# A hybrid decoder layer on one core: expert passes of 96 and 32 rows on four column tiles, two banks for head pairs, moved convolution taps, squares added ahead, and x transposed unscaled

## What is computed

```
h = rms_norm(x); proj = h @ w_in                     # conv value, conv gate, q, k, v
conv = silu(layer_norm(causal_conv31(value * sigmoid(gate))))    # 512 channels
attn = attention(rope(q), rope(k), v)                # 8 heads of 64, causal
x += concat(rms_norm(conv), rms_norm(attn)) @ w_out
h2 = rms_norm(x, g_ffn)
group = argmax(h2 @ w_group + b_group)               # 1 of 4
e1, e2 = top2(h2 @ w_erouter[group] + b)             # 2 of its 8 experts
x += sum of gate * (silu(h2 @ w_gate[e]) * (h2 @ w_up[e])) @ w_down[e]   # 32 experts, 1024 -> 256 -> 1024
x += (p @ w_ple) * sigmoid(rms_norm(x) @ w_ple_gate + b)
out = rms_norm(x, g_final)
```

## Time and profile before

| | us |
|---|---|
| median of 3 runs | 652.24 (651.92 to 652.33) |
| the profiled execution | 651.7 |
| its span, first to last instruction | 649.8 |
| PE busy in the span | 551.8 (85%) |
| DVE, ACT, POOL busy | 297.3, 185.7, 82.2 |
| mean granted PE clock | 0.945 of full speed |
| chain that ended last | PE 55%, DVE 19%, DMA 15%, ACT 7% |

### The profile page before, as it was taken

One profiled execution on the slowest core, in us unless ns is written; L12 is line 12 of the kernel. 1 busy time (PEld: TensorE's weight loads), 2 busy tenths in 40 slices (PEclk: granted clock), 3 DMA queues, 4 the chain that ended last, 5 costly groups with the idle time before them and its releaser, 6 DMA issues.

```text
span 649.8 us, 7753 instructions
## 1 busy us (share of the span) xinstructions
PE 551.8 (85%) x2628; PEld 322.9 (50%) x2629; DVE 297.3 (46%) x551; ACT 185.7 (29%) x348; POOL 82.2 (13%) x106
## 2 busy tenths in 40 slices
PE   1999999985779898897997889999999998729980
PEld 1788887753456687543332233333333332228870
DVE  3339868998872924474211111211121121175754
ACT  4831411346742432121101010110111010154554
POOL 0650000000000030002112012112211211000000
PEclk9999999996779989989999899999999999958995
DMA  8902102545004001664899998699899999265012
GB/s 342 384 3 72 67 9 58 219 144 211 1 0 195 1 1 66 266 283 168 323 418 419 421 421 348 235 419 385 335 417 422 368 421 419 119 259 210 2 43 86
DMA packets 34248, 145.86 MB, mean 224 GB/s; under 512 B 6576, under 2 KB 6832, under 8 KB 21808
## 3 DMA queue, kind: packets, MB, share of 16 engines
q1 hardware_dynamic: 27168, 133.70, 51.6%
q0 software_dynamic: 6480, 10.50, 4.4%
q10 hardware_dynamic: 576, 1.34, 0.5%
HBM read 142.90 MB, written 14.68 MB: 242 GB/s over the span
## 4 chain that ended last, share of the span: by engine, by line
PE 55%; DVE 19%; DMA 15%; ACT 7%; issue 2%; SPq 1%; POOL 0%; DVEq 0%; ACTq 0%; POOLq 0%
PE bank L1518 17%; DMA wring<-w_up_in 12%; PE bank L1266 10%; PE bank L1534 7%; DVE mix L888 6%; PE bank L1379 6%; PE bank L1563 2%; PE bank L1290 2%; DVE wring L946 2%; PE bank L1360 1%; PE bank L1497 1%; DMA c<-cst_in 1%; PE bank L1347 1%; PE bank L1444 1%; PE bank L1314 1%
## 5 line engine op out<-in xcount | busy, mean ns | idle before, releaser
L1518 PE MATMUL bank<-wring,arena 128*64 128x512 f32 x640 | 142.8, 599 | 13.7 <-SPq L506 12.0
L1518 PEld LDWEIGHTS bank<-wring,arena 128*64 128x64 f32 x640 | 46.2, 138 | 107.4 <-issue 90.1
L888 DVE SCALAR_TENSOR_TENSOR mix<-arena,pr,mix 128x512 f32<-128x512 f32 x120 | 81.5, 751 | 0.0
L1534 PE MATMUL bank<-wring,arena 128*64 128x512 f32 x320 | 73.1, 599 | 9.5 <-ACT arena L800 9.5
L1176 DVE TENSOR_TENSOR arena<-arena,bank 128x256 f32<-128x256 f32 x20 | 8.4, 422 | 148.7 <-ACT arena L797 148.7
L797 ACT ACTIVATE arena<-bank 128x256 f32<-128x256 f32 x20 | 7.7, 384 | 143.9 <-PE bank L1518 143.9
L1534 PEld LDWEIGHTS bank<-wring,arena 128*64 128x64 f32 x320 | 21.2, 136 | 48.5 <-issue 34.3
L1181 DVE COPY arena<-bank 128x512 f32<-128x512 f32 x20 | 13.8, 692 | 66.4 <-PE bank L1534 66.4
L1266 PE MATMUL bank<-hT_hi,win_hi 128*128 128x512 f32 x128 | 33.5, 398 | 1.5 <-DVE hT_lo L866 0.9
L803 ACT ACTIVATE arena<-bank 128x512 f32<-128x512 f32 x20 | 11.9, 597 | 75.8 <-PE bank L1534 75.8
L1266 PE MATMUL bank<-hT_lo,win_hi 128*128 128x512 f32 x128 | 31.6, 389 | 0.0
(11 more groups left out here) (203 smaller groups left out, 812.0 us busy)
## 6 DMA issues: line engine op xcount, KB each, us to landing
wring<-w_gate_in SPq DMA_DIRECT2D x32, 1024.0 KB, 10.4
wring<-w_up_in SPq DMA_DIRECT2D x32, 1024.0 KB, 12.7
wring<-w_down_in SPq DMA_DIRECT2D x32, 1024.0 KB, 15.6
wring<-w_in_in SPq DMA_DIRECT2D x5, 2048.0 KB, 19.1
wring<-w_out_in SPq DMA_DIRECT2D x2, 2048.0 KB, 8.0
wring<-y_d SPq DMA_DIRECT2D x8, 512.0 KB, 6.8
xs<-x_in SPq DMA_DIRECT2D x4, 512.0 KB, 7.5
xs<-x_in SPq DMA_DIRECT2D x1, 2048.0 KB, 8.0
```

Source lines behind the costliest of these rows:

```text
L888: ins = dve.scalar_tensor_tensor(out=mixc[:, mm, :], in0=u[:, mm, j:j + S], scalar=w, in1=mixc[:, mm, :], op0=ALU.mult, op1=ALU.add)
L1518: ins = pe.matmul(pb[2 + s][a * CAP:(a + 1) * CAP, :], xgT[:, s, k, a * CAP:(a + 1) * CAP], up_w(w, a)[:, :, k, :], start=(k == 0), stop=( ...
L1534: ins = pe.matmul(pb[6 + half][a * CAP:(a + 1) * CAP, :], hidT[:, s, k, a * CAP:(a + 1) * CAP], dn_w(w, a)[:, k, half * 512:(half + 1) * 5 ...
```

## The change

What it does, part by part (`...` marks what is left out):

- Expert passes have room for 96 rows of one expert and 32 of the other, on four column tiles of 32. In pairs 0 and 1 the even expert is the one with room for 96; in pairs 2 to 15 it is the one with more rows, and SP reads from `order` which expert's weights go into which half of the slot. Each matmul of a pass becomes four.
- The head pairs' outputs lie in banks 6 and 7 in turn. ACT does `probs_out` before `attn_out`, and the split of the convolution half's output weights after the loop.
- Taps: 71 are done before the first scores (66), then 7 in each of the first four units (as before), one in each later one (two), and the last 13 after the loop (6). The first `turn` comes after 57 taps (44).
- POOL adds up the squares of the head pairs, DVE those of the convolution blocks, so that one product per token tile sums them; DVE no longer reduces 16 sums.
- PE turns x as it is, right after its additions; the router's weights are multiplied by the gains once (`wr_scaled`), logits come out with tokens on partitions, and DVE applies the row's scale and the bias (which goes over memory to be spread over partitions). The normalised rows are still stored for the gathers, off this path; the last tile's after the choice of experts.
- `outa` uses banks 0, 1, 2, 6, 7, 0, 1, 2, `outc` banks q % 3; the mean comes after q = 2; w_pp is loaded after the last `outa`.

```diff
-GLU2, GLU3, TURN, EARLY = 20, 34, 54, 66
-TAPS_BY = (73, 80, 87, 94) + tuple(range(96, 120, 2))
+GLU2, GLU3, TURN, EARLY = 20, 34, 57, 71
+TAPS_BY = (78, 85, 92, 99) + tuple(range(100, 112))
-CAP = 64
+BIG, SMALL = 96, 32
+PARTS = tuple((lo, lo + SMALL, lo // BIG) for lo in range(0, P, SMALL))
+FIXED = 2
+FAR_ON = 64
-MOST = PAIRS + 2 * S // CAP
+MOST = PAIRS + 2 * S // SMALL
-STEPS = S // CAP - 1
+STEPS = S // SMALL - 1
...
-            banks.use(("attn", u // TT), 6)
-    banks.use("attn_sq", 7)
+            banks.use(("attn", u // TT), 6 + u // TT % 2)
+    banks.use("attn_sq", 4)
...
+            def expert(g, a):
+                if isinstance(g, int) and g < FIXED:
+                    return 2 * g + a
+                return number(sp, order[0:1, bass.ds(g, 1), a], 0, NE - 1)
...
-                                 src[bass.ds(2 * g + a, 1)].rearrange("e (p k) n -> p (e k) n", k=DK)
+                                 src[bass.ds(expert(g, a), 1)].rearrange("e (p k) n -> p (e k) n", k=DK)
...
+                if m >= 1:
+                    pool.wait_ge(sqa_ready, m + 1)
+                    wait(pool, sq_added, m - 1)
+                    pool.tensor_tensor(sqa[:, 0, :], sqa[:, 0, :], sqa[:, m, :], ALU.add).then_inc(sq_added, 1)
...
-                if u_ == 9:
-                    act.wait_ge(woc_loaded, 16)
-                if 9 <= u_ < 9 + CM:
-                    split_out(0, u_ - 9)
+                if u_ >= 2:
+                    probs_out(u_ - 2)
                 if u_ % TT == 3 and u_ > TT:
                     attn_out(u_ // TT - 1)
-                if u_ >= 2:
-                    probs_out(u_ - 2)
             attn_out(CM - 1)
...
+                banks.wait_full(act, ("h2", t, 1))
+                emptied(act.activation(hT[:, 4:8, t * P:(t + 1) * P], ..., ACT.Copy), ("h2", t, 1))
...
-            taps(GLU3 - 6, TURN - 10)
+            taps(GLU3 - 6, TURN)
             turn(0)
-            taps(TURN - 10, TURN)
+            dve.tensor_tensor(wr[:], wr[:], ..., ALU.mult).then_inc(wr_scaled, 1)
             taps(TURN, EARLY)
...
-            for q in range(2):
+            for q in range(3):
                 add_scaled(("outa", q), 1, q)
...
+            for m in range(1, CM):
+                dve.wait_ge(osq_ready, m + 1)
+                wait(dve, csq_added, m - 1)
+                dve.tensor_tensor(sqc[:, 0, :], sqc[:, 0, :], sqc[:, m, :], ALU.add).then_inc(csq_added, 1)
...
+            def logits_out(t):
+                banks.wait_full(dve, "logit")
+                return dve.scalar_tensor_tensor(out=lg[:, t, :], in0=bk("logit")[:, t * NR:(t + 1) * NR], scalar=rs[:, 1, t:t + 1],
+                                                in1=bias_row, op0=ALU.mult, op1=ALU.add)
...
+            scaled_rows(1, TT - 1)
...
-            chosen_value(SIDE, table8(C_SIDE, NE))
...
+            step(dve.tensor_copy(beyond[:], bk("count")[:, 0:NE]))
+            step(dve.tensor_tensor(larger[:, FIXED:, 0], pairs[:, FIXED:, 0], pairs[:, FIXED:, 1], ALU.is_ge))
+            step(dve.tensor_scalar(larger[:, FIXED:, 1], larger[:, FIXED:, 0], -1.0, 1.0, ALU.mult, ALU.add))
+            step(dve.tensor_scalar(pairs, larger[:], float(1 - BIG // SMALL), float(BIG // SMALL), ALU.mult, ALU.add))
+            emptied(dve.tensor_tensor(pairs, pairs, tokens, ALU.mult), "count")
...
+            step(dve.tensor_scalar(LOW, T0, float(FAR_ON), None, ALU.is_lt))
+            dve.scalar_tensor_tensor(out=H, in0=LOW, scalar=float(FAR_ON), in1=T0, op0=ALU.mult, op1=ALU.add)
+            step(dve.tensor_scalar(T1, LOW, float(BIG // SMALL - 1), 1.0, ALU.mult, ALU.add))
+            step(dve.tensor_tensor(T1, T1, R, ALU.mult))
+            step(dve.tensor_tensor(cmp8, over8(T1, STEPS), table8(C_THR, STEPS), ALU.is_ge))
+            step(dve.tensor_reduce(X, cmp8, AX.X, ALU.add))
+            dve.tensor_tensor(H, H, X, ALU.add)
+            step(dve.tensor_scalar(T1, LOW, float(SMALL - BIG), float(BIG), ALU.mult, ALU.add))
+            step(dve.tensor_tensor(T1, T1, X, ALU.mult))
+            step(dve.tensor_tensor(T1, R, T1, ALU.subtract))
+            step(dve.scalar_tensor_tensor(out=KEY, in0=LOW, scalar=float(BIG), in1=T1, op0=ALU.mult, op1=ALU.add))
...
-                    for m in range(CM):
-                        ins = pe.matmul(bk(name)[:, t:t + 1], src[:, m, t * P:(t + 1) * P], ones[:, 0:1],
-                                        start=(m == 0), stop=(m == CM - 1))
+                    ins = pe.matmul(bk(name)[:, t:t + 1], src[:, t * P:(t + 1) * P], ones[:, 0:1], start=True, stop=True)
...
-                if u_ >= 2 * TT and u_ % TT == 0:
-                    attn_squares(u_ // TT - 2)
...
+            def turn_rows(t):
+                for half in range(2):
+                    banks.wait_emptied(pe, ("outc", 2 * t + half))
+                rows = xs[:, t, :].rearrange("p (n k) -> p k n", k=DK)
...
+            def logits(t):
+                for k in range(DK):
+                    if k % 4 == 0:
+                        banks.wait_emptied(pe, ("h2", t, k // 4))
+                    ins = pe.matmul(bk("logit")[:, t * NR:(t + 1) * NR], hT[:, k, t * P:(t + 1) * P], wr[:, k, :],
+                                    start=(k == 0), stop=(k == DK - 1))
...
-                if q == 1:
+                if q == 2:
                     pe.wait_ge(tap_done, CM * TAPS)
                     mean_of("mean", mixc)
...
+                if q == 1:
+                    pe.wait_ge(csq_added, CM - 1)
+                    channel_sum("conv_sq", sqc[:, 0, :])
+                if half == 0 and t >= 1:
+                    turn_rows(t - 1)
                 if half == 1 and t >= 1:
-                    turn_rows("h2", t - 1, TT)
+                    logits(t - 1)
+            turn_rows(TT - 1)
+            logits(TT - 1)
...
                 for k in range(DK):
-                    for a in range(2):
-                        ins = pe.matmul(pb[2 + s][a * CAP:(a + 1) * CAP, :], xgT[:, s, k, a * CAP:(a + 1) * CAP],
-                                        up_w(w, a)[:, :, k, :], start=(k == 0), stop=(k == DK - 1))
+                    for lo, hi, a in PARTS:
+                        ins = pe.matmul(pb[2 + s][lo:hi, :], xgT[:, s, k, lo:hi], up_w(w, a)[:, :, k, :],
+                                        start=(k == 0), stop=(k == DK - 1))
```

202 lines of the change are left out of this document (93 added, 109 removed).

## The result

The changed kernel takes 635.66 us (median of 4 runs, 633.76 to 638.25); the kernel before, run beside it, takes 652.08 (650.49 to 652.33). The ratio is 0.976, with a 95% interval of 0.971 to 0.980: 16.4 us faster, where 29 were forecast and the range allowed 613 to 641. The profiled execution took 638.25 us, the slowest of the four; its span is 636.1, its mean granted clock 0.933.

A forecast was written before the change was run, and what follows sets the result against it. Bounds by stage: waits and lowered clock in attention, VectorE then PE in output projection, VectorE in routing, PE or transfers in the expert loop. Gains 17.2 + 10.6 - 3.1 + 4.4 took 651.7 to 622.6 us; range 613 to 641.

The forecast's parts named there:

- the two rivals with 640 and 630: 640: four tiles overlap imperfectly, 0.13 us a group, chance 0.08; 630: clock stays low in attention, chance 0.15.
- the main case: Whole kernel: all terms as summed, 622.6 us, with bounds 616 to 629; chance 0.66.
- Attention: Attention loop: two banks, ScalarE's order and moved taps end the last `attend` at 179.8 instead of 199.7, gain 19.9 us.
- the walk through the units: Attention loop from unit 8 to the last `attend`: following each score through its steps gives 26.7 us, plus 2.5 for clock.
- Mean and first `outc`: Output projection: the mean after q = 2 costs 2.7 us, so the first `outc` ends 17.2 us earlier.
- The new bank order only lets PE run ahead of it: nothing: Output projection: changed banks let PE run ahead of VectorE's chain from mean to scaled convolution, for no gain.
- Squares and x unscaled: From `outc` to logits: net gain 1.4 us inside `outc`, 9.2 behind it, together 10.6, bounds 7 and 12.
- Routing: Choice of experts: added small operations 2.1 us, longer thresholds and lists 1.0, cost 3.1 on the path, bounds 2 and 5.
- Four tiles: Expert passes: a group of four column tiles takes what two take, price 0, upper ends 0.17 and 0.44 us a group.
- that rival: Expert passes: four tiles overlap imperfectly, 0.13 us a group, a pass of 15.5, total 640; chance 0.08.
- The expert loop: Passes: 18 run instead of 20, last down product ends at 563.5 instead of 567.9, gain 4.4 us.
- transfers bind from pair 5 on: 375.5 + 10 x 16.2: Expert loop: last weights come at 537.5 at 16.2 us a pair, plus 1 for the pause at pair 7.

The follow-up runs named there:

- E1: The changed kernel with all head pairs' outputs back in bank 6; 645.64 us, ratio 0.985 to the kernel before.
- the second profile: The changed kernel run again unaltered, on another chip; 635.92 us, ratio 0.975 to the kernel before.
- E4: The kernel before with each matmul of a pass cut to run on four column tiles of 32, same rows and passes; 655.27 us, ratio 1.002.
- E5: The changed kernel with SyncE reading a pair's two expert numbers once instead of before each of six transfers; 634.81 us, ratio 0.974.
- E2: The changed kernel with the old tap schedule (44 before the first rotation, 66 before the first scores, two per later unit); 646.03 us, ratio 0.986.
- E12: The changed kernel with expert numbers read once, low weight parts split before the mean, 17 passes and seven unread products on PE; 619.54 us, ratio 0.951.
- E3: The changed kernel with the passes of before: 64 rows of each expert, two column tiles, 20 passes, shorter routing; 628.2 us, ratio 0.960.
- E7: The changed kernel with 17 passes, fixed for these inputs, instead of 18 run two by two; 624.22 us, ratio 0.957.
- E10: The changed kernel with passes of 64 and 64 rows and VectorE's low output-weight parts split before the mean; 625.68 us, ratio 0.959.

## Why the prediction was right in its direction and too large

The forecast's number was 13 us too low, and its range held. Of the signs that it named, one went against it: it called itself wrong if the loop lasted longer than 264 us, and the loop lasted 270.7. The measured time lies nearer to the two rivals with 640 and 630 than to the main case, but for other reasons than theirs: no product on four tiles was slower, and the clock in the attention loop was 0.93, not under 0.8.

**Attention (19.9 forecast, 18.9 measured): right.** The wait for bank 6 was the cause named, E1 brings it back with its lowered clock, and what was late next was the rotated rows, as forecast. The shares were not what I thought: undone alone, the bank costs 7.8 us, the taps 9, ScalarE's order 4.5. They add up to 21.3, more than 18.9, so they overlap. I had costed the moved taps by the earlier start of the loop alone; but the walk through the units, 26.7 us, rested on the small number of taps in them, and that is where most of the taps' worth was.

**Mean and first `outc` (17.2 forecast, 14.7 measured).** The mean came 16.0 us earlier, as the one product more costs 2.9. The step that failed is "The new bank order only lets PE run ahead of it: nothing", and with it the reading that VectorE's chain set this end before. The kernel before has no wait there (timelines of TensorE and ScalarE, before):

```profile
232.84 1.07 PE L1379 MATMUL bank<-woc_hi,mixc_hi 128*128 128x512 f32 x4
```

```profile
230.75 0.61 ACT L768 ACTIVATE mixc_hi<-mix 128x512 fp32r<-128x512 f32 x1
```

The scaled convolution was ready at 231.36, and PE came to it 1.5 us later, behind its own products. After the change PE has one product less between the mean and `outc`, is there first and waits 2.39 us. That wait is no loss: `outc` starts 23.8 us after the mean, where it was 25.4. The loss is in the first `outc` product, 5.6 us instead of 2.7, since it no longer finds its inputs ready: it waited 1.02 us for the low half, and at a lowered clock needed 1.67 and 2.08 us for what takes 1.07. In the second profile, with the full clock, it took 4.8, and the whole stage is 16.2 us earlier. So 1.5 of the 2.5 us missing here are the clock of one execution.

**Squares and x unscaled (10.6 forecast, 9.2 measured): right**, in size and form. A group of logits took 1.87 us against 1.8, a product by ones with 8 records 0.95 against 0.9, and no turn waited. In the second profile the same stretch gained 10.4. I did not run this part alone; it is read from the traces.

**Routing (3.1 forecast, 3.0 measured): right.** 254.55 to 272.77 is 18.2 us, before 278.48 to 293.65 was 15.2.

**Four tiles (nothing): right**, in the changed kernel and in E4: 7.07 us for 64 records, 0.44 for each group of four. The Trainium skill (TensorE: Matmul & The Clock Gate, Part 3, measured speedup) gives 3.07 times for four row tiles and 2.38 for three column tiles; with a group on four tiles at the time of one record on the whole array, the trace shows 4, so the measurement decides against that rival.

**The expert loop (4.4 us gained by forecast, 6.5 lost): wrong, and here lies the miss.** The loop from the first pass to the last down product lasts 270.7 us, before 264.2, and 259.8 was forecast. The 11 us too much are three terms of the sum:
- The reads, 1.1: the first load starts 8.5 us behind the first pass instead of 7.4. E5 gives it back (7.4).
- The transfers, 8.2: the step that failed is "transfers bind from pair 5 on: 375.5 + 10 x 16.2". I took one interval, 16.2 us, for the pace of all pairs, with 1 us for the pause at pair 7. From the first load to pair 15 it took 235.6 us against 227.4; in nine more profiles with these passes it took 234.9 to 237.8. The bytes agree (95.2 MB by the sum above, 95.07 before); at the 420 GB/s of an undisturbed slot they would need 227. The throughput line shows where the rest goes. Its first five slots, 310 to 389 but for one, miss 3.4 us; the two at pair 7, 341 and 295, 2.9; the last four, 385 to 253 but for one, 2.9. The dip at pair 7 is its second pass: the slot stays taken for 12.4 us longer, the queue runs empty, and the cost was three times my 1 us.
- The last two passes, 1.6: the clock was lowered in pair 15's up product (8.53 us). This term belongs to the one execution. In the second profile the two passes took 25.1 us, as forecast; there the first load came 10.2 us behind the first pass instead, after an up product of 8.77. The loop lasted 270.3 us.

The first slots' loss goes with PE's two pauses: pair 3's load comes 17.1 us after pair 2's (309.01), with a pass of 12.4. In E2 the pauses add up to 8.3 us, in E12 to 7.4, in the other eight profiles with these passes to 6.0 to 6.9; the longest two stretches from the first load to pair 15 are those of E2 (237.8 us) and E12 (236.2). The prediction had no such term. Nothing in the trace before shows one: its loop has no wait with `issue` as its end. What ties the pauses to the number of instructions: E4 doubles the matmuls alone, and two pauses of 8.6 us in sum appear; E3, with half the matmuls again, has one of 2.0; the changed kernel has two, 6.7. And the trace has a DMA queue that brings instructions, over the same engines that the weights fill. In the 4 us that hold the first pause, the queue for instructions brings one packet:

```profile
q8 instruction: 1, 0.02, 1.4%
```

One packet arrives in the second pause too, and one in each pause of E4. All 6 of that queue's packets in the loop arrive by 345 us, none in the 183 us after, and there are no pauses of this kind after 345. So the fit is with code that is brought when it runs for the first time, late, since the weights' transfers are ahead of it. This is argued, not shown: no run changed the fetching by itself. And two things speak against a simple form of it: the kernel before gets three such packets between 303 and 346 us without a pause, and E3's pause (317.4 to 319.45 us) holds none. Nor does that line say which engine a packet is for. The Trainium skill (Runtime: NRT & Kernel Launch, Instruction fetch mechanics) says that instructions come in blocks of 16 KiB, that PE holds 2048 instructions, and that the cost of a new block is mostly hidden. The size agrees (0.10 MB in 6 packets); if the pauses are such loads, their cost is not hidden here, with 2.8 to 4.8 us each in the changed kernel and E4. No run here shows how many instructions PE holds.

**The pass without rows.** Its 12.4 us were in the sum, and E7 shows 11 to 12 of them on the path. The sum said that the packing gains 4.4; it should have been set against its own routing (3.1) first, which leaves 1.3. That so little was left for so large a change was in the numbers, and I did not say it. With the loop's true terms it is a loss, 7 to 10 us by E3.

**The best version.** E12 takes 619.5 us, 16 less than the changed kernel. Its 17 passes are written for these inputs. Of the versions that take any routing, E10 has the lowest median, 625.7, with E3 at 628.2 not told apart from it.

## What to carry to other kernels

A loop that is bound by transfers gains little from less work on the engine beside it (here 8.5 to 9.2 us for three passes fewer ahead of the last pair, each of 12.4), and the passes behind the last transfer count almost in full. So look at the end of such a loop (an empty pass, two passes where one would do) before its middle. Take the pace of transfers from the longest stretch that the trace has, bytes over time, and price each place where the queue can run empty by its own slots in the throughput line, not by one good interval. And a gain of 1 or 2 us ahead of a stage can be hidden by the clock that the next products happen to get: look at their length, not only at their start, and profile the unchanged kernel twice before you lay such a difference to an edit.

## What was not expected of the hardware

- Doubling the matmul instructions of the loop cost nothing in the products (7.07 us in E4, 7.09 before) but brought pauses of 4.8 and 3.8 us early in the loop; the changed kernel's are 2.8 and 3.9 us, the first in the midst of a product.
- The same kernel, run twice, had its lowered clock in different products: the first up product took 7.07 us in one profile and 8.77 in the other, pair 15's 8.53 and 7.07.
- A register read on SyncE ahead of a transfer takes about 0.6 us: transfers start 1.14 us apart with it and 0.47 without.
